# Modulation columns dealt out 6 and 2 per trip instead of 4 and 4

## The reference

```python
def adaln(cvec, w, b):
    m = jax.nn.silu(cvec) @ w + b
    return jnp.split(m[:, None, :], N_MOD, axis=-1)

sh1, sc1, ga1, sh2, sc2, ga2 = adaln(c, w_mod[i], b_mod[i])
csh1, csc1, cga1, csh2, csc2, cga2 = adaln(c_ctx[None, :], w_mod[i], b_mod[i])
px = modulate(rms_norm(x, norm_mix[i]), sh1, sc1) @ w_in[i]
pc = modulate(rms_norm(xc, norm_mix[i]), csh1, csc1) @ w_in[i]
```

## Time and profile before

| | us |
|---|---|
| median of 3 runs | 3425.47 |
| lowest and highest | 3417.46, 3426.49 |
| profiled execution | 3431.14 |
| its span in the trace | 3429.3 |
| TensorE busy in the span | 3194.8 (93%) |
| VectorE, ScalarE busy | 2173.4 (63%), 1546.3 (45%) |

### The profile page before, as it was taken

One profiled execution on the slowest core, in us unless ns is written; L12 is line 12 of the kernel. 1 busy time (PEld: TensorE's weight loads), 2 busy tenths in 40 slices (PEclk: granted clock), 3 DMA queues, 4 the chain that ended last, 5 costly groups with the idle time before them and its releaser, 6 DMA issues.

```text
span 3429.3 us, 67500 instructions
## 1 busy us (share of the span) xinstructions
PE 3194.8 (93%) x29287; PEld 2758.0 (80%) x29287; DVE 2173.4 (63%) x3164; ACT 1546.3 (45%) x2090; POOL 225.4 (7%) x307
## 2 busy tenths in 40 slices
PE   6699998978888888989999999999889999999998
PEld 5578887767888777878888888888768888888887
DVE  5755556667677666665555556568777666666555
ACT  5544445544333333344444444345544444444333
POOL 1000000022222221000000000002110000000000
PEclk8899999999999999999999999999999999999999
DMA  9566668800000000655656555565435655656553
GB/s 324 161 200 211 197 199 275 279 15 7 7 7 7 7 7 4 203 160 184 190 180 192 186 187 184 183 211 162 140 112 176 192 182 187 189 180 190 184 190 129
DMA packets 549265, 529.86 MB, mean 155 GB/s; under 512 B 16916, under 2 KB 545706, under 8 KB 548074
## 3 DMA queue, kind: packets, MB, share of 16 engines
q1 hardware_dynamic: 546074, 516.08, 47.8%
q0 software_dynamic: 2832, 9.45, 0.8%
q10 hardware_dynamic: 64, 0.02, 0.0%
HBM read 521.28 MB, written 4.19 MB: 153 GB/s over the span
## 4 chain that ended last, share of the span: by engine, by line
PE 67%; DVE 9%; ACT 2%; issue 1%; POOL 0%; DVEq 0%; ACTq 0%
PE ps L1740 34%; PE ps L1741 17%; PE ps L1856 9%; PE ps L2072 2%; PE ps L2073 1%; DVE lo L1065 1%; PE ps L1876 1%; PE ps L1866 1%; PE ps L1864 1%; DVE L L1286 1%; DVE stB L1400 1%; DVE lw L1282 1%; DVE stB L1392 0%; ACT hi L747 0%; PE ps L1977 0%
## 5 line engine op out<-in xcount | busy, mean ns | idle before, releaser
L1065 DVE TENSOR_TENSOR lo<-raw,hi 128x1024 fp32r<-128x1024 f32 x936 | 1130.4, 1226 | 711.0 <-ACT hi L747 707.1
L1740 PE MATMUL ps<-mov,hi 128*128 128x512 f32 x4000 | 1427.1, 401 | 33.7 <-DVE lo L1065 21.5
L747 ACT ACTIVATE hi<-raw 128x1024 fp32r<-128x1024 f32 x936 | 972.6, 1055 | 862.1 <-PE ps L1741 614.3
L1741 PE MATMUL ps<-mov,lo 128*128 128x256 f32 x4000 | 1126.3, 282 | 0.0
L1740 PEld LDWEIGHTS ps<-mov,hi 128*128 128x128 f32 x4000 | 756.3, 189 | 227.4 <-DVE lo L1065 27.2
L1741 PEld LDWEIGHTS ps<-mov,lo 128*128 128x128 f32 x4000 | 760.2, 190 | 0.6 <-issue 0.5
L1740 PE MATMUL ps<-hid,hi 128*128 128x512 f32 x704 | 248.8, 399 | 0.0
L1774 PE MATMUL ps<-hi,c 128*32 128x256 f32 x768 | 193.2, 291 | 47.1 <-DVE lo L1065 46.7
L768 ACT ACTIVATE tmp<-ps 128x512 f32<-128x512 f32 x157 | 93.7, 597 | 284.2 <-PE ps L1741 260.3
L1741 PE MATMUL ps<-hid,lo 128*128 128x256 f32 x704 | 197.7, 281 | 0.0
L1775 PE MATMUL ps<-lo,c 128*32 128x256 f32 x768 | 188.9, 286 | 0.0
(11 more groups left out here) (342 smaller groups left out, 4271.4 us busy)
## 6 DMA issues: line engine op xcount, KB each, us to landing
raw<-in_w_in SPq DMA_DIRECT2D x184, 512.0 KB, 4.6
raw<-in_w_mod SPq DMA_DIRECT2D x160, 512.0 KB, 5.0
raw<-in_w_gate SPq DMA_DIRECT2D x88, 512.0 KB, 4.5
raw<-in_w_up SPq DMA_DIRECT2D x88, 512.0 KB, 4.5
raw<-in_w_down SPq DMA_DIRECT2D x88, 512.0 KB, 4.5
raw<-in_w_ffn_gate SPq DMA_DIRECT2D x88, 512.0 KB, 4.6
raw<-in_w_ffn_up SPq DMA_DIRECT2D x88, 512.0 KB, 4.6
raw<-in_w_ffn_down SPq DMA_DIRECT2D x88, 512.0 KB, 4.2
```

Source lines behind the costliest of these rows:

```text
L747: act.activation(hi[:, s, :, :], src, ACT.Copy).then_inc(hi_ready, 1)
L1065: dve.tensor_tensor(lo[:, s, :, :], raw_at(ph, i, j)[0], hi[:, s, :, :].bitcast(F32), ALU.subtract)\
L1740: pe.matmul(ps[:, b, :], hi[:, s, kk, w], moving(k, None), start=first, stop=False)
L1741: mm = pe.matmul(ps[:, b, 0:T], lo[:, s, kk, w], moving(k, 0), start=False, stop=last)
```

## The change

Before, each trip of `in_kv` and of `in_rest` multiplies 4 groups of modulation columns. After, a trip of `in_kv` multiplies 6, three in each half trip, behind product chunks 0, 1 and 2; a trip of `in_rest` multiplies 2, one in each half trip, behind product chunk 0. A half trip of `in_kv` is then c0, 4 side chunks, c1, 4 side chunks, c2, 4 side chunks, c3; one of `in_rest` is c0, 4 side chunks, c1, c2, c3. The columns go in the same order as before: groups 0 to 23 in `in_kv`, 24 to 31 in `in_rest`. The other edits keep the numbering of groups, the columns' addresses and the places of the bias addition in step.

```diff
-MOD0 = {"in_kv": 2, "in_rest": 4}
-SIDE = 4
+SIDES = {"in_kv": 6, "in_rest": 2}
+SIDES0 = {"in_kv": 0, "in_rest": 24}
...
-                if name in MOD0 and c % 2 == 0:
-                    self.order += [(True, 2 * p + c // 2, e) for e in range(n)]
+                per = SIDES.get(name, 0) // pairs
+                if c < per:
+                    self.order += [(True, per * p + c, e) for e in range(n)]
...
     def side(self, i, m):
-        return i * SIDE + (4 * SIDE * (self.name == "in_rest") + m + 1)
+        return self.side_index(i, m) + 1
+
+    def side_index(self, i, m):
+        return SIDES0[self.name] + i * SIDES[self.name] + m
...
-            return weights(A["w_mod"], q, i * (D // 2) + (MOD0[ph.name] * D + p * CN))
+            return weights(A["w_mod"], q, 2 * D + ph.side_index(i, p) * CN)
...
                         if pair and pair[0]:
-                            if pair[1] % 2:
+                            if pair[1]:
                                 mod_bias(ph, i, pair[1] - 1)
                             mod_row2(ph, i, pair[1])
                         elif pair:
                             evacuate(i, pair[1])
-                            if ph.name in MOD0:
-                                mod_bias(ph, i, 2 * pair[1] + 1)
+                            if ph.name in SIDES and pair[1] == ph.pairs - 1:
+                                mod_bias(ph, i, SIDES[ph.name] - 1)
...
             def mod_bias(ph, i, m):
-                n = i * 8 + (MOD0[ph.name] * KB + 2 * m)
+                n = 2 * KB + 2 * ph.side_index(i, m)
```

## The result

The changed kernel takes 3396.72 us (median of 20 runs, 3381.21 to 3413.78), the kernel before 3417.67 us (20 runs, 3396.16 to 3432.20): a ratio of 0.9935, 95% interval 0.9918 to 0.9951, so 17 to 28 us less. I had forecast 18.8 us less, and 3406.7 us with a range from 3398. The gain lies near the forecast. The time lies 10.0 us under the forecast and 1.3 us under the range: 7.8 us of the 10.0 are that the kernel before itself came out at 3417.67 and not at the 3425.47 from which I had worked, the other 2.2 that the medians lie 20.9 us apart and not 18.8. Both have to be explained, and the second turned out to be the more interesting.

The account below looks back on a forecast made before the run. TensorE was taken to bound in_kv, the weight feed in_rest. Matmul time +35.2 and -36.6 us, waits -24.4 with 7.0 remaining, gave -18.8 us: from the median 3425.5 to 3406.7 us, range 3398 to 3424.

Parts of the forecast that it names:

- Step 1: in_kv's matmuls: each half trip gains a group, its column matmuls and a dearer product, 4.40 us, times 8, +35.2 us.
- Step 2: in_kv's feed: four slots turn in 1.8 us per chunk, under the 1.99 asked, so 0 us of new wait.
- Rival A: in_kv: loads slow under denser demand and every new burst waits, 34 us on top, 3441 us; chance 0.08 in full.
- Steps 3 and 4: in_rest: 4.6 us less matmul time per half trip, -36.6 us; its 24.4 us of waits and slow clock shrink to 7.0.
- The sum: in_kv and in_rest together: +35.2 - 36.6 - 24.4 + 7.0 = -18.8 us; matmul time a wash, the gain the waits.
- rival B: in_rest: a group's wait belongs to its own burst, not missing loads; kept groups still lose 1.4 us, -12.1 us; chance 0.20.
- A sign that I set badly: in_rest, changed kernel's trace: ScalarE's waits for DMA were to be under 20 us.
- C: in_rest: all kept groups but the first run without waits and the clock stays up, -21.9 us, 3403.6 us; chance 0.13.

## Why the prediction was right, and its time was not

**Step 1, in_kv's matmuls.** Forecast +4.40 a half trip; measured 35.18 - 31.09 = +4.1 undisturbed and +4.37 with what waits there were. The term was mis-sized by 0.3: I took every product behind a group to cost 5.67, and where column matmuls stand in front of the group it costs 5.55, twice in a half trip; the group itself costs 3.73 there and not 3.77. Over the stage, 264.2 us before (153.58 to 417.80) and 299.9 after (152.03 to 451.90): +35.7 for +35.2. That these agree is luck: 8 x 4.1 is 32.7, another 1.9 are waits in two groups and the products behind them, and 0.9 is the stage's first product chunk (7.07 and 7.99 us, at a granted clock of 0.77 and 0.67), which takes 7.1 to 8.5 us in the five profiles of the two kernels. Over all profiles of the two kernels the stage is 265.2 us before and 299.2 after on the mean, +33.9.

**Step 2, in_kv's feed.** Forecast no new wait, with 0.35 us to spare at the tightest residue. Two groups waited by 0.7 and 0.8 us (at 264 and 431 us) in the one profile, none in the other. Loads landed in a median of 4.7 us, as before. Rival A did not come. The window of the earlier trace rows takes in 29 us of in_lora, as in_kv ends at 417.8; in the last seven half trips alone ScalarE waited 65.2 us for TensorE to free a slot before, and 39.9 us after. That ScalarE's waits for side chunks rose from 18.9 to 42.1 us shows how near the limit was: 237 GB/s here, and in_rest moved no more than 272 to 283 GB/s in the runs in which the feed bound it.

**Steps 3 and 4, in_rest.** The forecast was 187.9 - 36.6 - 24.4 + 7.0 = 133.9 us, measured 132.4 (133.2 in the second profile; of the 36.6, 4.6 times 8 is 36.8). What remains over 8 x 15.9 = 127.3 is 5.1 us for my 7.0: 2.3 in the first group and 1.5 at the end as forecast, the other seven groups 1.3 for 2.1, and slow clock none for 1.0. The halved loads show that the term was the right one: the waits were for loads, and the lost clock went with them. The 24.4 us were those of one execution: the kernel before took 187.9, 187.4 and 183.4 us for the stage in three.

**The sum.** -18.8 forecast; in the trace -19.4 (A: mean 530.0 before, 510.6 after). By the means of the profiles in_kv grew 1.3 us less than forecast, and in_rest fell by 0.6 us less (-53.4 for -54.0). The Trainium skill's price of a transfer ("DMA: Bandwidth & Descriptors", section "Anatomy of one DMA"), fitted for another engine's queue, is an estimate of 3.2 us for 512 KB. The traces don't agree: the earlier trace rows had 4.8, the changed kernel has 4.7, and the halved loads decided for the row and against rival B.

**A sign that I set badly.** I wrote that ScalarE would wait under 20 us for loads in in_rest; it waits 29.8 + 2.9. With halved loads in the changed kernel it still waits 28.1 us and the stage is as long. ScalarE's wait says only that it is ready before the load; whether that costs anything is said by TensorE's waits.

**The time.** Here the prediction failed, and the step is the last one, "below, C less the spread of the median of runs (some 5 us, as runs lie between 3417 and 3426)", together with the base. I had three runs, 3417.46, 3425.47 and 3426.49, and took their median for the kernel's, with 5 us for its scatter. The 20 runs of the kernel before lie in three clusters: one at 3396.2, twelve from 3412.5 to 3419.9 (mean 3415.9), seven from 3425.3 to 3432.2 (mean 3428.3). The clusters of several runs lie 12 to 13 us apart, near the 13 to 16 us between the two lengths of a stretch, and two stretches of two lengths each give three clusters.

The three profiled runs of the kernel before bear this out: with both stretches long they took 3431.1 and 3430.1 us, with one short 3421.1, though in_rest took 187.4 us in that one. So what the profiled execution had over the median was not more waits in in_rest, as I had thought possible. Two of my three runs were of the upper cluster.

In the changed kernel the clusters are five runs from 3381.2 to 3386.5, ten from 3393.3 to 3401.5 (mean 3396.9) and five from 3405.4 to 3413.8 (mean 3409.7). Cluster against cluster the change is worth 19.0 and 18.7 us. A median of three could move by a whole cluster either way, so some 14 us and not 5 should have stood at both ends, or the range should have been set on the difference.

The kernel before with half loads shows the same from the other side: seven of its ten runs lie from 3400.1 to 3405.0, where 16 us under the middle cluster should be, three higher and none in a lowest one, while ten of the 31 runs of the kernel before beside it were below 3406. So its ratio is only 0.9977 where the trace has 16.0 us (514.0 for 530.0). Why its runs fell so isn't known; with ten runs it may be chance.

What decides the pace of a stretch wasn't found, and no experiment was made on it. It isn't the kernel's text, as one kernel shows both, and it isn't waits, as TensorE has no gap in either; that loads play no part is not shown. It holds from the start of a stage over hundreds of us, and in the changed kernel's profile the output projection in front ran at 290 matmuls per 50 us and the feed-forward stage behind the norm at 285.

## What to carry to other kernels

Work that costs matmul time anywhere belongs beside the stage whose feed has slack: 8 groups cost 33 to 37 us of matmul time in either stage, and the gain was mostly the waits that they had caused in the one. Price a ring by its turn (load, split, residue, over the number of slots) and compare it with the time per chunk that the schedule asks for in its densest stretch, not over the stage. Before a time is forecast to 0.3%, look at whether the runs lie in clusters; if they do, forecast the difference, and compare traces over the stretch that the change touches.

## What the runs showed of the hardware

The same stream of matmuls with TensorE never idle, at granted clock 1.00, ran at one of two paces, 0.353 or 0.346 us for a pair of 512 and 256 columns, and kept it over hundreds of us; two such stretches account for some 30 us of scatter between runs of one kernel. A load of 512 KB took 4.7 to 5.2 us to land in the median, with no rise to be seen from 203 to 283 GB/s in the stage (4.8 us at both), and one of 256 KB 3.1 us. And a small block can change its neighbours: behind four matmuls of 2 columns the next group took 3.73 us and not 3.77, and the product behind that 5.55 and not 5.67.
